# Value pages of a paged attention loaded as 64 partitions of 8 KB instead of 128 partitions of 4 KB

## The reference, cut to what matters

```python
k_past = cache_k[l][page_table]      # 8 sequences, 16 pages each, 128 keys of 8 heads x 128
v_past = cache_v[l][page_table]      # the same for the values
s_past = jnp.einsum('bqhmd,bkhmd->bhmqk', q, k_past)          # two maps m of 64 features
sc = jnp.concatenate([s_past, s_new], axis=-1) * scale
w = diff_weights(sc + alibi_bias(qpos, kpos), lam)            # softmax(map 0) - lam * softmax(map 1)
out = einsum('bhqk,bkhd->bqhd', w[..., :p], v_past) + einsum('bhqk,bkhd->bqhd', w[..., p:], v_new)
```

## Time and profile before

| | |
|---|---|
| median of three runs | 2714.27 us (2712.66 to 2714.98) |
| the profiled execution, time | 2711.31 us |
| its span, first to last instruction | 2709.5 us |
| PE busy | 2611.9 us (96%) |
| DVE / ACT / POOL busy | 1497.4 / 942.0 / 354.3 us |
| bytes moved by DMA | 506.37 MB, of them 67.1 MB keys and 67.1 MB values (128 transfers of 512 KB each) |
| mean granted TensorE clock | 0.989 |

### The profile page before, as it was taken

The page is one execution under the profiler, slowest core; times in us unless marked ns, Lnnn a source line. Parts: engine busy times, 40 slices in busy tenths (PEclk is TensorE's granted clock), DMA queues, the critical chain, the costliest instruction groups (busy, mean ns, idle before and its releaser), DMA issues.

```text
span 2709.5 us, 49989 instructions
## 1 busy us (share of the span) xinstructions
PE 2611.9 (96%) x20082; PEld 2542.3 (94%) x20082; DVE 1497.4 (55%) x2082; ACT 942.0 (35%) x1075; POOL 354.3 (13%) x630
## 2 busy tenths in 40 slices
PE   7999999999999999988887899999999999999997
PEld 7999999999999999977775899999999999999997
DVE  5555555555555644467786345555555555555655
ACT  5222322223222332354555433222222222222433
POOL 2000000000000120066865010000000000000323
PEclk9999999999999999999999999999999999999998
DMA  5444444444444455799999844444444444444342
GB/s 231 156 143 152 155 141 153 146 149 154 145 149 152 142 185 200 284 377 365 377 375 382 305 155 144 152 150 145 155 147 147 154 142 153 151 143 155 140 145 81
DMA packets 92112, 506.37 MB, mean 187 GB/s; under 512 B 10401, under 2 KB 10402, under 8 KB 51298
## 3 DMA queue, kind: packets, MB, share of 16 engines
q1 hardware_dynamic: 90866, 496.59, 50.5%
q0 software_dynamic: 1136, 8.32, 0.9%
HBM read 495.63 MB, written 9.23 MB: 186 GB/s over the span
## 4 chain that ended last, share of the span: by engine, by line
PE 89%; DMA 3%; ACT 2%; SPq 2%; issue 2%; POOL 1%; DVE 1%; POOLq 0%; DVEq 0%; ACTq 0%
PE bank L1589 26%; PE bank L1590 26%; PE bank L1591 26%; PE bank L1675 2%; PE bank L1677 2%; PE bank L1676 2%; DMA raw<-k_pool 2%; PE bank L1715 1%; PE bank L1764 1%; SPq L427 1%; POOL ssq L518 1%; SPq L422 1%; PE bank L1741 1%; ACT x_hi L666 1%; DMA raw<-v_pool 1%
## 5 line engine op out<-in xcount | busy, mean ns | idle before, releaser
L1589 PE MATMUL bank<-x_hi,w_hi 128*128 128x320 f32 x3584 | 1111.6, 310 | 17.0 <-DVE w_lo L1046 10.9
L1590 PE MATMUL bank<-x_lo,w_hi 128*128 128x320 f32 x3584 | 1109.9, 310 | 0.0
L1591 PE MATMUL bank<-x_hi,w_lo 128*128 128x320 f32 x3584 | 1109.7, 310 | 0.0
L1037 DVE TENSOR_TENSOR w_lo<-raw,w_hi 128x2048 fp32r<-128x2048 f32 x309 | 707.7, 2290 | 305.8 <-ACT w_hi L648 291.0
L648 ACT CAST w_hi<-raw 128x2048 fp32r<-128x2048 f32 x294 | 559.6, 1903 | 838.2 <-PE bank L1591 838.2
L1589 PEld LDWEIGHTS bank<-x_hi,w_hi 128*128 128x128 f32 x3584 | 674.9, 188 | 19.0 <-issue 13.6
L1590 PEld LDWEIGHTS bank<-x_lo,w_hi 128*128 128x128 f32 x3584 | 675.1, 188 | 0.2
L1591 PEld LDWEIGHTS bank<-x_hi,w_lo 128*128 128x128 f32 x3584 | 674.9, 188 | 0.0
L1589 PE MATMUL bank<-mid_hi,w_hi 128*128 128x320 f32 x1408 | 435.3, 309 | 1.0 <-DVE w_lo L1037 1.0
L1591 PE MATMUL bank<-mid_hi,w_lo 128*128 128x320 f32 x1408 | 435.1, 309 | 0.0
L1590 PE MATMUL bank<-mid_lo,w_hi 128*128 128x320 f32 x1408 | 435.1, 309 | 0.0
(11 more groups left out here) (215 smaller groups left out, 2011.7 us busy)
## 6 DMA issues: line engine op xcount, KB each, us to landing
raw<-slabs_ffn SPq DMA_DIRECT2D x264, 1024.0 KB, 4.7
raw<-k_pool SPq DMA_DIRECT2D x128, 512.0 KB, 6.5
raw<-v_pool SPq DMA_DIRECT2D x128, 512.0 KB, 6.4
raw<-slabs_in SPq DMA_DIRECT2D x48, 512.0 KB, 7.8
raw<-slabs_ple SPq DMA_DIRECT2D x18, 1024.0 KB, 4.8
raw<-slabs_in SPq DMA_DIRECT2D x16, 1024.0 KB, 4.8
raw<-slabs_out SPq DMA_DIRECT2D x16, 1024.0 KB, 4.8
h<-x_t SPq DMA_DIRECT2D x4, 640.0 KB, 8.1
```

Of the source, the lines that this page charges most:

```text
L1037: vt.tensor_tensor(w_lo[n % 2][:, :, :], raw[n % 4][:, :].rearrange("p (k n) -> p k n", n=P), w_hi[n % 2][:, :, :].bitcast(F32), ALU.subtr ...
L1589: mm(out, w_hi[w2][:, t, :], xh, start=start, stop=False)
L1590: mm(out, w_hi[w2][:, t, :], xl, start=False, stop=False)
L1591: return mm(out, w_lo[w2][:, t, :], xh, start=False, stop=stop)
```

## The change

A page of values is now moved to half of the partitions. Page `e` of an item goes to partitions 64e to 64e + 63, and each of these gets two neighbouring values of the page, 8 KB that lie together in memory: 64 rows of 8 KB in place of 128 rows of 4 KB. The bytes, the number of transfers, their order, their semaphores and the waits before them are as before. Pages of keys are loaded as before.

In the slot, partition 64e + k now holds value 2k of page e in its first 4 KB and value 2k + 1 in its second. So the scores must come in that order: `score` reads the keys of the two pages as even keys of page 0, even keys of page 1, then odd keys of page 0 and of page 1. That is, its 256 columns are read in four runs of 64 with a step of two elements (8 bytes) within a run. The positions in `kloc` are generated in the same order, by one iota with four dimensions. `turn`, `weigh` and all else are untouched, and on every engine the instructions stand in the same order, one for one.

```diff
-            def two_pages(pool, pages_, slot):
+            def key_pages(pages_, slot):
                 for e, page in enumerate(pages_):
                     sp.dma_start(ring[slot][:, 1024 * e:1024 * e + 1024],
-                                 pool[bass.ds(page, 1), :, :].rearrange("o p n -> (o p) n")
+                                 k_pool[bass.ds(page, 1), :, :].rearrange("o p n -> (o p) n")
+                                 ).then_inc(ring_in[slot][e], 16)
+
+            def value_pages(pages_, slot):
+
+                for e, page in enumerate(pages_):
+                    sp.dma_start(ring[slot][QD * e:QD * e + QD, :],
+                                 v_pool[bass.ds(page, 1), :, :].rearrange("o (p r) n -> (o p) (r n)", r=2)
                                  ).then_inc(ring_in[slot][e], 16)
...
-                    two_pages(k_pool if kind == "K" else v_pool, pages_, slot)
+                    (key_pages if kind == "K" else value_pages)(pages_, slot)
...
-            nc.gpsimd.iota(kloc[:, :], [[1, 512]], base=0, channel_multiplier=0,
+            nc.gpsimd.iota(kloc[:, :].rearrange("p (m r e k) -> p m r e k", m=2, r=2, e=2),
+                           [[2 * P, 2], [1, 2], [P, 2], [2, QD]], base=0, channel_multiplier=0,
...
                             e = mm(K_BANK[half][32 * j:32 * j + 32, 256 * e2:256 * e2 + 256],
-                                   Qb[b % 2][:, 4 * half + j, :], keys[:, :, 4 * half + j, :], start=True, stop=True)
+                                   Qb[b % 2][:, 4 * half + j, :],
+                                   keys[:, :, 4 * half + j, :].rearrange("p e (k r) -> p r e k", r=2),
+                                   start=True, stop=True)
```

## The result

| | before | changed |
|---|---|---|
| median | 2714.26 us (2712.66 to 2714.98, 4 runs) | 2873.88 us (2863.56 to 2883.45, 4 runs) |
| the profiled execution, time / span | 2711.31 / 2709.5 us | 2863.56 / 2861.8 us |
| PE busy | 2611.9 us | 2678.5 us |
| mean granted TensorE clock | 0.989 | 0.955 |

What follows compares the result with a forecast made beforehand. DMA throughput was taken to bound the attention part, PE the FFN parts. Half the partitions +98 us and larger rows -1 us, all else 0, gave +97 us: 2714.3 + 97 = 2811 us, range 2765 to 2892.

Steps and rivals of the forecast that it cites:

- (a): Queue of the 16 engines: all stay in step, each values page pays the full half-partition loss, +131 to +178 us; chance 0.26.
- What bounds, and where the loss falls: Attention part, 1134 to 1515 us: DMA throughput bounds (99% busy), so costlier values pages reach the end one for one.
- Half the partitions: Values' transfers: 64 partitions move at 217 GB/s, as a store did; +131 us in full, +98 us after a quarter avoided.
- 0.75 x 131 = +98 us: Values' transfers: half-partition loss of 131 us, a quarter taken as avoided by engines a part of a page apart.
- Larger rows: Values' transfers: rows of 8 KB at 424 GB/s against 409 would give -6 us; a quarter counted, -1 us.
- Keys with a step of two: PE in `score`: reading keys with a step costs 0 at the end; bounds nothing or +58 us of PE.
- Scores and positions: `kloc` iota in POOL, and bias, maxima, exponentials and transposes: same elements and shapes, 0.
- SP: SP's queue: same count of issues and waits, pairs of pages issued well within their transfer time, 0.
- packets under 8 KB: Sign in the DMA counts: fewer of these, by 16384 less the 8192 of 8 KB that replace them.
- (b): Queue of the 16 engines: halves interleave fully, only the gain of 8 KB rows is left, -6 us, 2708; chance 0.13.
- (c): PE in the attention part: granted clock falls and bounds, adding only below 0.64; a mixture +150 to +210 us; chance 0.06.
- (d): Values' transfers: rows of 8 KB cut into 4 KB packets, the forecast with 1 us more; no chance of its own.

Runs made afterwards that it cites:

- parity run: Changed kernel with page e at every second partition (2k + e) and keys' columns read alternately from the two pages: 2727.42 us, ratio 1.0049 to the kernel before.
- run over the middle: Changed kernel with page 0 at partitions 32 to 95, page 1 in two transfers to 0 to 31 and 96 to 127: 2824.19 us, ratio 1.0404.
- parity run with no cost of PE: Pages at every second partition, keys read as in the change, matmul writing its bank with a step of two: 2714.85 us, ratio 1.0003 to the kernel before.
- keys and values in turn: Changed kernel with items ordered keys, values, keys, values instead of keys, keys, values, values: 2945.67 us, ratio 1.086 to the kernel before.
- control of the run over the middle: Changed kernel with page 0 at partitions 0 to 63, page 1 in two transfers to 64 to 95 and 96 to 127: 2880.79 us, ratio 1.0625.

## Why the prediction was right, and where its size was off

**The number.** 2873.88 us lies in the range of 2765 to 2892, but 63 us above the forecast of 2811 and above the forecast's own range, 2774 to 2845. The range held because it took in rival (a).

**What bounds, and where the loss falls: right.** The attention part is bound by the throughput of the DMA engines, and a loss there reached the end one for one: 153 us longer in the stretch, 152 us in the span.

**Half the partitions: right mechanism.** The store of 64 partitions at 217 GB/s was the right row: values alone move at 239 GB/s in the change and 224 in rows of 4 KB, and at 411 once each page spreads over the height of the buffer. That a store reads SBUF and a load writes it made little difference. By the Trainium skill (SBUF — State Buffer, "Door 1: The DMA port swizzle") the lower and the upper 64 partitions have disjoint ports, and by its formula every second partition reaches all 16. The parity run agrees with that (411 GB/s); the run over the middle agrees with it in direction only.

**"0.75 x 131 = +98 us": the term that was mis-sized, in two ways.** First, a quarter of the loss was taken off for engines out of step. In the last pass that is about right: at 239 GB/s the values would take 67.1 MB / 239 = 281 us, 103 us more than 178. Over the whole stretch it is too much. There the packets of 8 KB take 0.571 us on the mean (8422 packets, nearly all of them values), so the 8192 of the values cost 8192 x 0.571 / 16 = 292 us of the 16 engines; before, their 16384 packets of 4 KB at 0.171 us cost 175. That is **117 us**, nine tenths of the 131 and not three quarters. Why the values fare worse between keys than alone (0.571 against 0.55 us) stays open.

Second, the term took the values alone and put every other transfer at nothing. The 17728 packets of 4 KB that are not values (keys, projection slabs and a few stores) take 0.198 us on the mean where packets of 4 KB took 0.171 before: 17728 x 0.027 / 16 = **30 us**. Together that is 147 of the 153 us by which the stretch grew; the other 6 us are not broken down. The single packets show what the 30 us depend on, half pages in flight beside them, and the parity run, where it is gone, that their place is the cause.

**Larger rows, -1 us: small, as forecast.** One transfer of 1 MB gives 4 to 5 us, where the rates gave 6; in the parity run with no cost of PE nothing was left of it.

**Keys with a step of two, 0: right**: 2713.91 us with that half alone. *Scores and positions, SP: 0*, likewise within that run.

**A sign misread.** The prediction wanted the packets under 8 KB to fall "by 16384 less the 8192 of 8 KB that replace them". The new ones are not under 8 KB, so the fall is the whole 16384; 8192 is the fall of all packets.

**The rivals.** (a), all engines in step, +131 to +178 us, gave the time that came (+160), and by its reason only in part. For the values it came near: 0.571 us for 8 KB is 230 GB/s over the stretch, against its 217. But the rate depends on how often the half changes, which engines in step would not show, and the 30 us on the other transfers it did not have either. (b) fell: the halves do not interleave fully by themselves. (c), the clock: it fell to 0.79 in the stretch, but PE stayed at 73% busy and waited 132 us for pages, so it did not bound, as the bound of 0.64 said. (d) fell with the count of packets.

## What to carry to other kernels

In this kernel the number of partitions of a transfer did not tell its speed, their place did: before a load goes to a part of the buffer, look for a transfer of that shape in the trace, and divide the engines' busy time by the packets in a window where it is alone. When a transfer becomes slow, price its neighbours in the same queue as well: here a full-width packet took nearly twice as long beside half pages, 0.317 us instead of 0.165. If a layout must use 64 partitions, try every second one: it cost the DMA side nothing here (411 against 409 GB/s), and the reordering that it needs could be hidden in the step of a matmul's output.

## What was not expected of the hardware

Changing the half more often was faster up to a point: 274 GB/s with transfers of 32 partitions in turn against 239 with 64, although there were twice as many transfers, but 211 with 16. Transfers that nobody touched slowed down beside half pages, from 0.165 to as much as 0.317 us a packet. A matmul that writes its bank with a step of 8 bytes took 387 ns, the same as without, while one whose moving columns lie 4 KB apart took 497. The changed kernel's four runs spread over 0.7% (2863.56 to 2883.45 us), the four of the kernel before over 0.1%, and 23 of it on another chip over 0.3%. Other kernels with half pages spread over 0.1% (keys and values in turn) to 1.0% (the control of the run over the middle); what the spread depends on was not tried. And the order of items in the ring, with the same transfers, was worth 149 us.
